# Row sums of the first normalisation, both gelu tiles ahead of the gates, and a series on GpSimd, in an inference step of a hybrid decoder

## Chip, cores and metric

One core of a Trainium2 chip. The metric is the device time of one launch in microseconds (us). Three runs of the kernel before took 2537.53, 2539.8 and 2540.2 us; the median is 2539.8 us.

## The reference

One step of a two-layer decoder trunk for T = 1088 tokens (1024 of a prompt and 8 requests of 8 tokens), D = 1024, everything in float32. Layer 0 is a recurrent block:

```
xn = x * rsqrt(mean(x*x) + eps) * a_norm
gate, xb = split(xn @ w_in)                 # 1024 and 1024 columns
xc = causal depthwise conv of width 4 (xb)
r = sigmoid(xc_block @ gate_r_w[b] + gate_r_b)      # 4 blocks of 256 channels
i = sigmoid(xc_block @ gate_i_w[b] + gate_i_b)
log_a = -8 * r * softplus(-lambda);  a = exp(log_a)
b = sqrt(-expm1(2*log_a)) * (i * xc)
h[t] = a[t] * h[t-1] + b[t]
x = x + (gelu(gate) * h) @ w_out
```

Behind it stand a gated ConvFFN of 3072 channels, a shared K/V projection, a sliding-window attention layer and a second ConvFFN. The change touches the first normalisation and the recurrent block.

## The kernel before

**Layout and products.** x lies transposed in SBUF: 8 tiles of 128 channels by 1088 tokens (`x[:, k, :]`), in three chunks of 384, 384 and 320 tokens. Each float32 product is made of three: weights and data are both split into a rounded part (ScalarE, `Copy` into fp32r, lines 1360, 1365 and 1386) and a remainder (a subtraction on VectorE, lines 1866, 1871 and 1907), and TensorE adds hi x hi, hi x lo and lo x hi (lines 866 to 868). `piece(n, s, c)` is one chunk for 128 output columns, 24 matmuls; `unit(n, s)` is its three chunks. `s` is one of two sides: side 0 has weights `whi[0]`, `wlo[0]` and PSUM banks 0 to 2, side 1 has banks 3 to 5. `n` counts the weights of a side. `prep(n, s)` on ScalarE rounds the weights as soon as the last piece that used the old ones is done; `prep` on VectorE makes the remainder. SP fetches the next raw weights once the remainder is made.

**Queues.** There is no scheduler. Each engine has one hand-written list of instructions with semaphore waits, in which an instruction waits for all ahead of it in its own list. So the place of a `prep` or of a copy in ScalarE's list decides when TensorE gets it.

**Start.** SP loads six tiles of 128 tokens (512 KB each), then 18 small parameter rows, the first two weights (512 KB each), three more token tiles and ten small rows for the FFN. TensorE transposes each token tile in two halves (`set_up`, line 853), ScalarE and VectorE copy the halves alternately into `x` (lines 1354 and 1862). The mean of squares of a chunk is made in parts: ScalarE squares 4 or 6 of its 8 tiles (line 1404), GpSimd adds them (lines 2495 and 2498), VectorE squares and adds the rest (lines 1920 and 1923), and a matmul with a matrix of 1/D adds over the partitions (lines 901 and 903). ScalarE takes the root (line 1379), VectorE the reciprocal (line 1876), both over 128x384. Then for each of the 8 tiles VectorE multiplies x by the gain and the inverse root (line 1899), ScalarE rounds, VectorE subtracts (line 1907), and TensorE's `first_pair` follows tile by tile. The parameter transposes (line 839) and those of the FFN rows (line 845) stand between its pieces.

**A recurrent block c of four** (`lru_block`; blocks 1 and 2 are a loop with the block number in a register). TensorE: the two units of xb (n = 4c, sides 0 and 1), the unit of gate tile 2c (n = 4c+1, side 0), the gates r and i of both halves (four times three pieces of 6 matmuls, 72 together), then the unit of gate tile 2c+1 (n = 4c+3, side 1). ScalarE moves xb into `convin` (line 1444), VectorE makes the convolution (lines 2001 and 2003), ScalarE rounds it and VectorE takes the remainder `xclo` (line 2020), once for each half; both have to be there for the gates. ScalarE then has gelu (line 1462), four sigmoids (line 1482), two tanh (line 1492), two exponentials (line 1498) and two roots (line 1502), VectorE products and the scan (line 2051), and GpSimd the product with gelu (line 2537). Before block 0 VectorE computes softplus of lambda with a series of nine terms on 128x8 (lines 1958 to 1985), and GpSimd writes the history of each convolution into `convin` (line 2506).

**Last block and output projection.** ScalarE takes the last gate tile out of PSUM as it is, and applies gelu later (line 1531). Between the roots it rounds the six finished tiles of z in three chunks (line 1513); VectorE makes the remainders of three tiles of the first two chunks (line 2056), GpSimd the others (line 2526). TensorE runs six of the eight tiles of the output projection for all six banks, then the last two tiles bank by bank (lines 990 to 992). `residual` then adds into x (line 2108), squares, rounds x (line 1556) and only then the next weights.

`first_pair` of the KV and query projections uses a normalisation in which VectorE and GpSimd (line 2470) make the remainders in turn; the change extends this to the first one.

## Time and profile before

| | |
|---|---|
| median of three runs | 2539.8 us |
| the profiled execution | 2541.68 us, span 2539.8 us |
| TensorE matmul | 2477.2 us, 98% of the span, mean granted clock 0.987 |
| VectorE | 1276.9 us, 50% |
| ScalarE | 780.7 us, 31% |
| GpSimd | 250.8 us, 10% |
| DMA | 52 GB/s over the span |

The granted clock is a share of full speed, 2.4 GHz; 0.50 is the lower level, 1.2 GHz. In the profile PE is TensorE's matmul, PEld its weight load, DVE VectorE, ACT ScalarE, POOL GpSimd. A row names line, engine, operation, output <- inputs and shape. In rows by group "x12 | 6.3, 521" is the count, the busy time in us and the mean of one in ns; in rows in order of time the first two numbers are start and busy time in us, and a bracket tells how long the engine had been idle and what released it.

### The profile page before, as it was taken

Reading aid. Unit: us, or ns where it says so; the run is one execution under the profiler, and the core shown is the slowest. Engines: PE = TensorE matmul, PEld = TensorE weight load, DVE = VectorE, ACT = ScalarE, POOL = GpSimd, SP = SyncE. Lnnn points to the kernel's source line nnn. Section 1 sums busy time; section 2 is a strip of 40 time slices with the busy share of each in tenths; the row PEclk is TensorE's granted clock in tenths of the full one; section 3 lists DMA queues with packets and bytes.
Section 4 is the critical chain, followed back from the end, with each engine's and each line's share of the span. In section 5 each row is a group of like instructions: output and inputs, shape, how many; then the busy total and the mean of one; then the engine's idle time right before and its main releaser. Section 6 shows DMA issues by size and latency. Waiting matters only on the chain.

```text
span 2539.8 us, 39942 instructions
## 1 busy us (share of the span) xinstructions
PE 2477.2 (98%) x15280; PEld 2418.2 (95%) x15280; DVE 1276.9 (50%) x2054; ACT 780.7 (31%) x1266; POOL 250.8 (10%) x358
## 2 busy tenths in 40 slices
PE   5899999999999999999999989999999999999999
PEld 4899999999999999999999956999999999999999
DVE  7666645442443444345456667454434524533543
ACT  3554523221221221112334476332112202311221
POOL 2012241000000000000310054310000000000000
PEclk7999989999999999999999999999999999999999
DMA  3111111111111111111164112111111111111113
GB/s 110 38 42 41 50 34 42 50 34 50 50 37 46 50 41 37 54 41 42 50 144 100 49 37 88 42 51 41 37 54 41 36 55 41 41 41 50 46 35 93
DMA packets 227170, 130.89 MB, mean 52 GB/s; under 512 B 24781, under 2 KB 224653, under 8 KB 226860
## 3 DMA queue, kind: packets, MB, share of 16 engines
q1 hardware_dynamic: 224932, 126.47, 17.0%
q10 hardware_dynamic: 2100, 3.37, 1.1%
q8 instruction: 49, 0.80, 0.1%
q14 instruction: 25, 0.20, 0.0%
q0 software_dynamic: 64, 0.05, 0.0%
HBM read 116.76 MB, written 15.01 MB: 52 GB/s over the span
## 4 chain that ended last, share of the span: by engine, by line
PE 93%; DVE 4%; ACT 1%; issue 1%; POOL 0%; DMA 0%; DVEq 0%; ACTq 0%; POOLq 0%
PE ps L866 29%; PE ps L868 29%; PE ps L867 29%; PE ps L1199 1%; PE ps L1251 1%; PE ps L1116 0%; PE ps L901 0%; DVE y L2003 0%; PE ps L1084 0%; PE ps L1109 0%; PE ps L1299 0%; DVE sa L1907 0%; PE ps L1029 0%; PE ps L1301 0%; PE ps L1300 0%
## 5 line engine op out<-in xcount | busy, mean ns | idle before, releaser
L866 PE MATMUL ps<-sa,whi 128*128 128x384 f32 (+1 forms) x1836 | 603.5, 329 | 20.2 <-DVE sa L1907 13.1
L868 PE MATMUL ps<-sa,wlo 128*128 128x384 f32 (+1 forms) x1836 | 601.6, 328 | 0.0
L867 PE MATMUL ps<-sa,whi 128*128 128x384 f32 (+1 forms) x1836 | 601.3, 327 | 0.0
L866 PE MATMUL ps<-sb,whi 128*128 128x384 f32 (+1 forms) x1764 | 582.2, 330 | 0.0
L868 PE MATMUL ps<-sb,wlo 128*128 128x384 f32 (+1 forms) x1764 | 576.5, 327 | 0.0
L867 PE MATMUL ps<-sb,whi 128*128 128x384 f32 (+1 forms) x1764 | 576.1, 327 | 0.0
L1360 ACT ACTIVATE whi<-raw 128x1024 fp32r<-128x1024 f32 (+1 forms) x204 | 201.4, 987 | 836.7 <-PE ps L868 824.2
L866 PEld LDWEIGHTS ps<-sa,whi 128*128 128x128 f32 x1836 | 346.4, 189 | 23.3 <-issue 16.7
L867 PEld LDWEIGHTS ps<-sa,whi 128*128 128x128 f32 x1836 | 346.6, 189 | 0.5 <-issue 0.2
L868 PEld LDWEIGHTS ps<-sa,wlo 128*128 128x128 f32 x1836 | 346.6, 189 | 0.0
L866 PEld LDWEIGHTS ps<-sb,whi 128*128 128x128 f32 x1764 | 332.0, 188 | 2.8 <-issue 1.2
L867 PEld LDWEIGHTS ps<-sb,whi 128*128 128x128 f32 x1764 | 331.9, 188 | 1.4
L868 PEld LDWEIGHTS ps<-sb,wlo 128*128 128x128 f32 x1764 | 331.8, 188 | 0.0
L1866 DVE TENSOR_TENSOR wlo<-raw,whi 128x1024 fp32r<-128x1024 f32 (+1 forms) x204 | 235.0, 1152 | 161.9 <-ACT whi L1360 161.8
L2108 DVE TENSOR_TENSOR x<-ps,x 128x384 f32 (+3 forms) x216 | 115.3, 534 | 382.7 <-PE ps L868 377.5
L866 PE MATMUL ps<-sc,whi 128*128 128x384 f32 (+1 forms) x816 | 266.4, 326 | 2.6 <-DVE sc L1907 2.6
L868 PE MATMUL ps<-sc,wlo 128*128 128x384 f32 (+1 forms) x816 | 265.8, 326 | 0.0
L867 PE MATMUL ps<-sc,whi 128*128 128x384 f32 (+1 forms) x816 | 265.8, 326 | 0.0
L2177 DVE TENSOR_TENSOR convin<-ps,rstd 128x384 f32<-128x384 f32 x144 | 73.3, 510 | 213.6 <-PE ps L868 212.1
L2555 POOL COPY fstash<-convin 128x2 f32 x48 | 8.9, 185 | 1509.6 <-DVE y L2003 1509.6
L866 PEld LDWEIGHTS ps<-sc,whi 128*128 128x128 f32 x816 | 153.3, 188 | 4.5 <-DVE sc L1907 4.3
L867 PEld LDWEIGHTS ps<-sc,whi 128*128 128x128 f32 x816 | 153.2, 188 | 0.1
(338 smaller groups left out, 2596.3 us busy)
## 6 DMA issues: line engine op xcount, KB each, us to landing
raw<-in_f_w_up SPq DMA_DIRECT2D x96, 512.0 KB, 3.8
raw<-in_f_w_down SPq DMA_DIRECT2D x64, 384.0 KB, 3.4
raw<-in_a_w_in SPq DMA_DIRECT2D x16, 512.0 KB, 4.0
x_spill<-x SPq DMA_DIRECT2D x1, 4352.0 KB, 15.4
x<-x_spill SPq DMA_DIRECT2D x8, 544.0 KB, 5.5
xrows<-in_x_prompt SPq DMA_DIRECT2D x8, 512.0 KB, 6.5
raw<-in_a_w_out SPq DMA_DIRECT2D x8, 512.0 KB, 3.7
raw<-in_w_q SPq DMA_DIRECT2D x16, 256.0 KB, 3.6
```

The lines of the kernel that those rows point to most:

```text
L866: pe.matmul(out, whi[s][:, w], mhi[k][:, chunk(c)], start=(k == 0), stop=False)
L867: pe.matmul(out, whi[s][:, w], mlo[k][:, chunk(c)], start=False, stop=False)
L868: last = pe.matmul(out, wlo[s][:, w], mhi[k][:, chunk(c)], start=False, stop=(k == nk - 1))
L1199: last[e] = pe.matmul(out, qz[h0:h0 + HD, 4 * a + j, b * WIN:(b + 1) * WIN], kf[h0:h0 + HD, a, key:key + 256 - k0], start=True, stop=True)
L1251: last = pe.matmul(ps[h0:h0 + HD, 6, :], v, pt_buffer(2 * p + e)[:, h, :], start=(h == 0 or b == 0), stop=(h == 1))
L1360: act.activation(whi[s][:, 0:cols], raw[s][:, 0:cols], ACT.Copy).then_inc(hi_ready[s], 1)
L1866: dve.tensor_tensor(wlo[s][:, 0:cols], raw[s][:, 0:cols], whi[s][:, 0:cols].bitcast(F32), ALU.subtract)\
L2108: ins = dve.tensor_tensor(xt, bank(b, c), xt, ALU.add)
L2177: dve.tensor_tensor(gp[:, FFN_W - 1 + lo:FFN_W - 1 + lo + w], ps[:, c, 0:w], rstd[:, lo:lo + w], ALU.mult)\
L2555: pool.tensor_copy(fstash[:, ds(f, 1), 0:2], gp[:, SEQ:SEQ + 2].rearrange("p (o w) -> p o w", o=1))
```

## The change

*Start.* SP loads token tiles 0 to 2, a_norm as 8 rows of 128 (`anrow`), the first two weights, then token tiles 3 to 8, and the parameter rows behind them. ScalarE squares each token tile where it landed, tokens on partitions, with the sum over its 1024 channels accumulated into one column; a root of three columns and a reciprocal of three columns follow, and TensorE multiplies each column, broadcast to 128, with the identity, which puts the inverse roots of a chunk as a row on all partitions of a PSUM bank. VectorE's multiply reads them there. The remainders of odd tiles go to GpSimd. A first square root on one column loads the table. The transposes of a chunk's tokens stand one chunk ahead of its pieces; those of the FFN rows behind the whole pair.

*Blocks 0 and 3* (`both`). The unit of gate tile 2c+1 moves ahead of the gates (n = 4c+1, side 1). r uses side 0 and i side 1. Each tanh follows its r. Next weights of both sides are prepared in the second half of the gates. In block 3 the roundings of the six finished tiles follow each gelu piece, all 18 remainders are made on GpSimd, and gelu is applied straight from PSUM. The output projection's last two tiles go tile by tile over all banks, and its first residual rounds the next weights ahead of x.

*Series.* VectorE computes only exp(-|lambda|)/(2 + exp(-|lambda|)); GpSimd does the rest in block 0. GpSimd also writes the next block's history ahead of its wait for the second scan.

The diff, cut to its core (`...` marks what is left out):

```diff
+            for tt in range(3):
+                token_rows(tt)
+            eng.dma_start(anrow[:, :], A["a_norm"].rearrange("o (k p) -> (o k) p", p=P)).then_inc(an_in, 16)
+            conv_loads(0)
+            for tt in range(3, 9):
                 token_rows(tt)
             parameter_rows()
...
+            def root_spread(c):
+                pe.wait_ge(in_inv, c + 1)
...
+                for tt in range(3 * c, 3 * c + 3):
+                    w = P if tt < 8 else NS
+                    last = pe.matmul(ps[:, 6 + c % 2, (tt - 3 * c) * P:(tt - 3 * c) * P + w],
+                                     in_sums[0:w, tt:tt + 1].broadcast_to([w, P]), ident[0:w, 0:w], start=True, stop=True)
+                last.then_inc(in_spread, 1)
+            def first_products():
+                set_up(0, SET_END[0])
+                pe.wait_ge(an_in, 16)
+                pe.transpose(ps[:, 7, 0:KD], anrow[:, :], ident[0:KD, 0:KD]).then_inc(an_tr, 1)
+                root_spread(0)
+                set_up(SET_END[0], SET_END[1])
+                for c in range(3):
+                    for s in range(2):
...
+                        def ready(c, k):
+                            if (c, k) == (1, KD - 2):
+                                root_spread(2)
+                            normed(0)(c, k)
+                        piece(0, s, c, KD, split_a, None if s else ready)
+                        if (c, s) == (0, 0):
+                            root_spread(1)
+                            set_up(SET_END[1], SET_END[2] - 2)
...
+                pe.wait_ge(xn_mult, 3 * KD)
+                set_up(SET_END[2] + 2, NSET)
...
                 unit(4 * c + 1, 0, KD, split_a)
+                if both:
+                    unit(4 * c + 1, 1, KD, split_a)
                 pe.wait_ge(xc_lo, 2 * c + 2)
                 for m in range(2):
+                    for s, n in ((0, 4 * c + 2), (1, 4 * c + 2)) if both else ((1, 4 * c + 1), (0, 4 * c + 2)):
...
+            for c in range(3):
+                for s in range(2):
+                    out_part(s, c, range(KD - 2))
+            for k in range(KD - 2, KD):
+                for s in range(2):
+                    for c in range(3):
+                        out_part(s, c, [k])
...
+            def row_squares(tt):
+                w = P if tt < 8 else NS
+                wait(act, sq_done, tt)
+                act.wait_ge(rows_in[tt], 16)
+                act.activation(t1[0:w, 0:D], xrows[0:w, tt, :], ACT.Square, accum_out=in_sums[0:w, tt:tt + 1]).then_inc(sq_done, 1)
...
+            act.activation(spt[:, 0, 0:1], epst[:, 0:1], ACT.Sqrt)
+            row_squares(0)
+            set_up(0, 1)
+            row_squares(1)
+            set_up(2, 3)
+            row_squares(2)
+            row_roots(0)
+            set_up(4, 5)
+            prep(0, 0, KD * P)
             def first_chunk_in(k):
+                if k in (1, 3, 5):
+                    row_squares((k - 1) // 2 + 3)
+                elif k in (2, 4, 6):
+                    set_up(SET_END[0] + k - 2, SET_END[0] + k - 1)
+                if k == 6:
+                    row_roots(1)
+                elif k == 7:
                     prep(0, 1, KD * P)
...
             act.activation(spt[:, 1, :], spt[:, 0, :], ACT.Exp, scale=-1.0).then_inc(sp_exp, 1)
+            set_up(SET_END[2] + 2, NSET)
...
                         if ch == 1:
                             prepare()
+                        if last and s == 1:
+                            highs(ch)
...
                 branch(0, 4 * c + 1, lambda: prep_gates(4 * c + 2, 0))
+                if both:
+                    branch(1, 4 * c + 1, lambda: prep_gates(4 * c + 2, 1))
...
+                if both:
+                    act.wait_ge(sp_done, 2)
...
+                        if both and i == 0:
+                            act.wait_ge(bank_free[s * 3 + 2], n + 1)
+                            tanh(m)
...
-            with act.Fori(0, KD // 2 - 1) as i:
+            residual(N_OUT, 0, 1, C_FN, sb, KD * P, "", weights_first=True)
+            with act.Fori(1, KD // 2 - 1) as i:
...
+                def times(j, out):
+                    return dve.scalar_tensor_tensor(out, x[:, j, chunk(c)], an[:, j:j + 1], bank(6 + c % 2, c),
+                                                    ALU.mult, ALU.mult)
+                norm(0, c, split_a, times, between)
...
+            def softplus():
+                t, t2_, u = spt[:, 0, :], spt[:, 1, :], spt[:, 3, :]
+                pool.wait_ge(sp_ready, 2)
+                seq.mark(pool.tensor_tensor(t2_, t, t, ALU.mult))
+                seq.settle()
...
+                for i in range(terms - 2, -1, -1):
+                    seq.mark(pool.tensor_tensor(u, u, t2_, ALU.mult))
+                    seq.settle()
+                    seq.mark(pool.tensor_scalar(u, u, 1.0 / (2 * i + 1), None, ALU.add))
+                    seq.settle()
```

## Rows read from the trace of the kernel before

**Rows 1.** Waits of TensorE: who for whom; us in total, times, longest

```profile
PE ps L866 <- DVE sa L1907: 13.1, 4, 8.6
...
PE ps L866 <- DVE xclo L2020: 5.0, 1, 5.0
...
PE ps L866 <- DVE wlo L1866: 4.0, 1, 4.0
...
PE ps L866 <- issue: 3.0, 1, 3.0
```

**Rows 2.** Stretches: length; busy us (count) per engine; clock, DMA share, GB/s

```profile
0.00:83.16 83.16, 50.51 (x261) 42.79 (x261) 63.31 (x113) 33.89 (x65) 17.53 (x25) 0.82 0.28 85
83.16:126.50 43.34, 38.35 (x217) 38.09 (x218) 25.84 (x31) 24.99 (x34) 0.54 (x3) 0.92 0.21 56
...
100.22:114.70 14.48, 14.48 (x74) 14.48 (x75) 1.92 (x2) 9.99 (x17) 0.00 (x0) 0.82 0.13 36
281.13:293.00 11.87, 11.87 (x74) 11.87 (x73) 1.92 (x2) 9.08 (x15) 0.00 (x0) 1.00 0.15 44
307.50:341.75 34.25, 25.06 (x132) 23.50 (x130) 25.88 (x23) 15.66 (x26) 22.91 (x19) 0.89 0.05 16
...
341.75:347.60 5.85, 5.85 (x18) 5.85 (x19) 3.03 (x5) 3.37 (x5) 2.82 (x3) 0.50 0.32 90
```

**Rows 3.** TensorE in order of time, 0 to 75 us

```profile
4.57 7.95 PE L853 MATMUL ps<-ident,xrows 128*128 128x128 f32 x48 [4.57 <-DMA xrows<-in_x_prompt]
...
29.84 0.66 PE L866 MATMUL ps<-sa,whi 128*128 128x384 f32 x1 [8.57 <-DVE sa L1907]
```

**Rows 4.** Groups by shape, ScalarE and VectorE, 0 to 170 us (accumulator read: 1500 to 1700)

```profile
L1360 ACT ACTIVATE whi<-raw 128x1024 fp32r<-128x1024 f32 x7 | 7.4, 1058 | 0.6 <-PE ps L868 0.6
L1386 ACT ACTIVATE sa<-y 128x384 fp32r<-128x384 f32 x12 | 6.3, 521 | 12.5 <-DVE y L1899 12.5
...
L1354 ACT ACTIVATE x<-ps 128x512 f32<-128x512 f32 x8 | 4.4, 593 | 3.8 <-PE ps L853 3.8
...
L1815 ACT ACTIVATION_READ_ACCUMULATOR t<-t,stat 128x1 f32 x36 | 6.8, 188 | 0.0
...
L1866 DVE TENSOR_TENSOR wlo<-raw,whi 128x1024 fp32r<-128x1024 f32 x7 | 8.9, 1277 | 12.8 <-ACT whi L1360 12.7
L1862 DVE COPY x<-ps 128x512 f32<-128x512 f32 x8 | 5.2, 678 | 7.0 <-PE ps L853 7.0
...
L1907 DVE TENSOR_TENSOR sc<-y,sc 128x384 fp32r<-128x384 f32 x4 | 2.1, 556 | 6.1 <-ACT sc L1386 6.1
```

**Rows 5.** VectorE and GpSimd in order of time, later normalisation, 1342 to 1347 us

```profile
1342.05 1.61 DVE L1899 SCALAR_TENSOR_TENSOR y<-x,pcol,rstd 128x320 f32<-128x320 f32 x2
...
1345.93 1.12 DVE L2285 SCALAR_TENSOR_TENSOR kf<-kf,qkn,ps 128x384 f32<-128x384 f32 x2
...
1346.26 0.88 POOL L2470 TENSOR_TENSOR sc<-convin,sc 128x320 fp32r<-128x320 f32 x1 [1.00 <-ACT sc L1386]
```

**Rows 6.** ScalarE in order of time, behind the first block's tanh

```profile
118.66 1.28 ACT L1498 ACT_TABLE_LOAD   x1
119.95 1.21 ACT L1498 ACTIVATE t<-t,sp 128x1088 f32<-128x1088 f32 x1
```

**Rows 7.** VectorE in order of time: first convolution, second remainder, second scan of block 0

```profile
82.97 1.03 DVE L2001 TENSOR_SCALAR y<-convin,pcol 128x1024 f32<-128x1024 f32 x2
...
98.87 1.29 DVE L2020 TENSOR_TENSOR xclo<-y,xchi 128x1088 fp32r<-128x1088 f32 x1 [1.18 <-ACT xchi L1455]
...
134.47 2.47 DVE L2051 TENSOR_TENSOR_SCAN z<-z 128x1088 f32<-128x1088 f32 x1
```

**Rows 8.** ScalarE in order of time from 301 us; GpSimd groups by shape, 0 to 350 us

```profile
301.06 2.58 ACT L1513 ACTIVATE sa<-z 128x384 fp32r<-128x384 f32 x6
...
L2526 POOL TENSOR_TENSOR sa<-z,sa 128x384 fp32r<-128x384 f32 x6 | 9.1, 1541 | 37.6 <-ACT sa L1513 37.6
...
L2538 POOL COPY pcol<-z x2 | 2.4, 1194 | 0.0
```

More of the change, by code:

```diff
@@ L234, in build @@
         sp_ready = sem("sp_ready")
+        sp_done = sem("sp_done")
         hist_ready = sem("hist_ready")
@@ L967, in lru_block @@
                             piece(n + m, s, ch, 2, xc_split, k0=2 * m)
[L968 to L971 removed]
+                if not both:
+                    unit(4 * c + 3, 1, KD, split_a)
+            lru_block(0, first=True, both=True)
+            with pe.Fori(1, LRU_BLOCKS - 1) as c:
                 lru_block(c)
[L974 to L994 removed]
@@ new lines, in _, with out_part @@
+            lru_block(LRU_BLOCKS - 1, both=True)
+            def out_part(s, c, ks):
+                if ks[0] == 0:
+                    if c == 0:
+                        pe.wait_ge(hi_ready[s], N_OUT + 1)
+                        pe.wait_ge(lo_ready[s], N_OUT + 1)
+                    pe.wait_ge(bank_free[3 * s + c], N_OUT)
+                for k in ks:
+                    if k < KD - 2:
+                        pe.wait_ge(z_lo_pool, (KD - 2) * c + k + 1)
+                    else:
+                        pe.wait_ge(z_lo, k - (KD - 2) + 1)
+                    w, out = ds(k * P, P), bank(3 * s + c, c)
+                    zhi, zlo = split_a[0][k][:, chunk(c)], split_a[1][k][:, chunk(c)]
+                    pe.matmul(out, whi[s][:, w], zhi, start=(k == 0), stop=False)
+                    pe.matmul(out, whi[s][:, w], zlo, start=False, stop=False)
+                    last = pe.matmul(out, wlo[s][:, w], zhi, start=False, stop=(k == KD - 1))
+                if ks[-1] == KD - 1:
+                    last.then_inc(bank_ready[3 * s + c], 1)
@@ L1388, in norm_hi @@
                             between(k)
[L1389 to L1392 removed]
+                if chunks[-1] == 2:
                     act.wait_ge(xn_lo, lo_base(u + 1))
[L1395 to L1405 removed]
@@ L1444, in evac_conv, with lru_block @@
                     act.activation(gp[:, hist + lo:hist + lo + w], ps[:, b, 0:w], ACT.Copy).then_inc(bank_free[b], 1)
-            def lru_block(c, last):
+            def lru_block(c, first=False, last=False):
+                both = first or last
                 for s in range(2):
@@ L1455, in lru_block, with highs @@
                     act.activation(xchi[:, s, :], y[:, :], ACT.Copy).then_inc(xc_hi, 1)
+                def highs(ch):
+                    for k in range(KD - 2):
+                        act.wait_ge(z_ready, k + 1)
+                        act.activation(split_a[0][k][:, chunk(ch)], z[:, k, chunk(ch)], ACT.Copy).then_inc(z_hi, 1)
                 def branch(s, n, prepare):
@@ L2009, in conv, with lru_block @@
                         seq.settle()
-            def lru_block(c, last, start):
+            def lru_block(c, start, first=False, last=False):
+                both = first or last
                 seq.at = start
@@ L2530, in lru_block @@
                     h = gate_tiles(c, m)[1]
+                    if m == 1 and not last:
+                        conv_history(kt + 1)
                     pool.wait_ge(scan_done, kt + 1)
```

542 lines of the change are left out of this document (231 added, 311 removed).

## The prediction

> **What bounds the kernel now.** I began with the share of busy time (given above): TensorE at 98%, so what can be won is only its idle time, about 62 us, and its time at half clock. TensorE's waits say where the idle time lies [rows 1]: the longest are all in the first 102 us, plus two around the output projection of the recurrent block. The stretches show the clock [rows 2]: 0.82 on average up to 83.16 us, 0.82 again in the gates of the first block, 0.50 for 5.85 us behind the gap that ends at 341.75 us, and 1.00 where nothing waits. Of 72 small-operand matmuls, a unit or a block's gates, one takes 11.87 us at full clock (74 records there), so 0.165 us each; at half clock 0.325 us (18 in 5.85). Three stalls matter. (a) From 12.5 to 29.84 us TensorE has almost no work: the transposes of rows 0 to 5 end at 12.5 us and the first product starts at 29.84 us [rows 3]; between them lie squares, adds, a ones-matmul, root and reciprocal. Up to 80 us it goes on in pieces (13.1 us of waits for split tiles). (b) It waits 3.0 us at 79.9 us (the weight split stands on VectorE behind the softplus series) and 5.0 us at 95.2 us for the second half of the convolved input, then runs at half clock. (c) From 307.5 to 341.75 us TensorE is busy for 25.06 of 34.25 us at 0.89: 9.2 us idle, 3.8 us of clock, and 2.9 us of clock behind it, some 16 us.
>
> **Part 1, first normalisation.** It removes the squares by tile, their adds, the ones-matmuls and the wide reciprocals, and puts in nine row squares with accumulation, small roots and reciprocals, and nine 128-column matmuls that spread the inverses. No row shows a 128x1024 square with accumulation. Lower bound: the 128x1024 copy, 1.06 us; upper: that plus twice the accumulator read of 0.19 us [rows 4]. I take 1.25 us. No row has the multiply with the inverse in PSUM. Next to it: a DVE operation of this kind with a PSUM operand took 0.56 us beside a running GpSimd subtraction, while with both operands in SBUF it took 0.80 us in the same surroundings (two in 1.61 us, and of 320 columns only) [rows 5]. I take 0.56 and keep 0.8 for the range.
> The chain, from the durations of [rows 4]: row 0 lands at 4.5 us as now; three squares (3.75) and two copies (1.2) on ScalarE, roots, reciprocals and spread (0.9): the inverses are there at 10.3 us. Weights are queued ahead of rows 3 to 8; at one 512 KB tile in 1.33 us, which is what 48 transposes in 7.95 us imply, row 5 lands near 14 us, which hides. VectorE's chunk 0 is 8 multiplies, 4 subtractions, 2 weight splits of 1.23 us and 3 copies of 0.68 us: 11.2 us. ScalarE has 8x0.52 + 3x1.25 + 3x0.59 + 2x1.06 = 11.8 us. They alternate, so about 13.6 us: chunk 0 is done at 24 us. TensorE has to do all transposes of rows 3 to 5 before its first piece, and two of these hang on copies that stand at tiles 2 and 3 of the chunk: first product at 17.5 us, 12 us sooner than now. I let it run at half clock for 5 us, like behind other gaps. Piece to 24.5, spread and four transpose jobs (3.2), second piece 4.0: 31.5 us. Chunk 1 starts at 25 us and is bound by ScalarE (9.7 us and its waits): 36 us. TensorE: 37, then 41.3 us; the third chunk is done by 43-45 us, and two pieces of 320 columns with the parameter transposes end at 49.6, the f transposes at 51.3 us. Then a tail that the change itself makes: ScalarE copies those transposes only then (0.6 us), moves the convolution's input out of PSUM (four copies, 0.4 us each), and rounds the next weights (1.06); VectorE splits them (1.2); with 0.1 us for each hand-over 4 us behind 51.3. Second unit at 55.3 us; now it starts at 83.16 us. For subtractions that still collide with GpSimd I add 1 us: 56.3. **Term A: -26.9 us.** The moved DMAs cost nothing here: the parameter rows are wanted at 41 us, and the queue would have issued them by 14 us.
>
> **Part 2, series on GpSimd and both gelu tiles ahead.** The second unit is followed by the other gelu unit, so 23.7 us of matmuls cover both convolutions, which took from 82.97 to 100.16 us [rows 7]. Their 5.0 us wait and the half clock behind it go. From the second unit to the end of gates and both gelu units it is 43.3 us now (83.16 to 126.5), then 3 x 11.87 = 35.6. **Term B: -7.7 us.** The series on GpSimd: 23 dependent small operations from about 64 us. Below: 0.19 us plus a hand-over of 0.1, 7 us; above: 1.19 us each, as a one-column copy takes beside a busy VectorE [rows 8], 27 us. The first sigmoid wants it at 81 us. VectorE is idle in parts of that stretch, so I take 12 us: hidden, 5 us to spare. At the upper bound it would cost 10 us.
> **What is late next.** The gelu unit that stood behind the gates covered the scans. Now the next block's units follow at once. Its gates start 35.6 us after these gates end. VectorE's chain: second scan ends at 136.9 us, 22.2 us behind the gates' end at 114.7 [rows 7]; the tanh tiles now lie between the sigmoids, so the exponential starts 2.9 instead of 5.25 us behind [rows 6]: 19.8. Weight split 1.2, then two convolutions as at 82.97 to 100.16, 17.2 us: 38.2 us, and 0.6 for register-addressed operations. **Term C: +3.2 us** of wait; the bounds are 0 (the whole chain 3 us shorter) and 8 (another 2 us, and half clock behind it). I add 1 us for the clock.
>
> **Part 3, last block.** ScalarE now has the roundings of six tiles behind each gelu piece: 2.58 us for six [rows 8]. The rounding of the gate weights stands ahead of the second group and waits for the unit's end, 11.9 us, so the groups end at 17.8 us from the unit's start, the sigmoid table and first sigmoid at 19.7; the third set of gates waits 2.0 us for its bank. Behind the gates 1.4 us for the first weights and 0.7 for the second. GpSimd has all 18 subtractions, at 1.54 us beside VectorE [rows 8] 28 us, wanted piece by piece up to 39.6 us: hidden. The scan chain gives the seventh tile at 49.1 us, when six tiles' products (17.8 us) have ended at 45.6: 3.5 us idle and 2.3 us of half clock. The eighth tile is ready when wanted. With rounding of the weights first, the next unit starts about 1 us behind. Sum: 47.4 us of matmuls and 12.7 us of loss, 60.1 us. Now: 60.6 us (281.13 to 341.75) and 2.9 us of half clock behind it, 63.5. **Term D: -3.4 us.**
> On this chain lie table loads. The row shows 1.28 us, and the exponential begins 0.01 us behind it [rows 6]. The Trainium skill (ScalarE: Activation LUTs, What ACT_TABLE_LOAD costs) counts a drain of 1.38 us on top of each load, 2.66 us in all. By that rule the sigmoid and exponential loads of this chain would add 2.8 us and the sum would end at 2508.8 us; the trace does not agree, so I don't take it.
>
> **Sum.** -26.9 - 7.7 + 3.2 + 1 - 3.4 = -33.8 us. The profiled execution took 2541.7 us, which gives 2507.9; that execution lies 1.9 us above the median of the runs, 2539.8, and set against the median the change gives 2506.0 us, which I forecast. A measurement of this kernel tells 0.2%, 5 us, from no change.
>
> **Rivals.**
> *The start is less loose than drawn* (0.20). Multiplies are stretched to 0.8 us, squares take 1.44 us, and the pieces of the first chunk wait more: 24 x 0.24 + 9 x 0.19 = 7.5 us, and the second unit's clock falls back once more, 3 us; with term C at its upper bound 4 more. -19 us: 2521. For it: beside GpSimd the multiplies of the later normalisation are stretched [rows 5]. Against: their second operand will be in PSUM, and ScalarE, not VectorE, sets the second chunk.
> *Handover and last block go smoothly* (0.17). No wait at the second block's gates and no half clock in the last block: 4.2 + 2.3 us, and the first allowance of 1 us: -41 to -46, 2498 to 2494.
> *Slower: the clock never comes back while the start is in pieces* (0.04). Place: TensorE from 17.5 us to the gates of the first block. At 0.325 instead of 0.165 us a matmul the first pair ends 25 us later and the two units take 23.7 us more: -33.8 + 48.7 = +15 us, 2555. It decides once about 34 us' worth of full-clock work is done at half clock. Against it: behind 341.75 us half clock ended after 5.85 us, and the first block's gates got 0.82 in the mean [rows 2].
> *It doesn't do what it says* (0.05): the transposes ahead of the first piece, or the series, hold the first sigmoid as long as the old chain did, 10 us for the series and 15 for the transposes: -9 us, 2531.
> The forecast's own case has 0.54 (2500 to 2512). The range 2493 to 2521 leaves out the slow case, the one in which it does not do what it says, and the ends of the others. Faster by over 0.2%: 0.94; within: 0.02; slower: 0.04.
>
> **What would show it.** In the changed profile: first product near 17.5 us and second unit near 56 us (A); no wait for the convolved input in the first block (B); a new wait of 2 to 5 us of TensorE for it near 127 us, at the second block's gates (C); near 296 us two waits under 4 us at the last tiles of the output projection, and the next weights' wait down from 4.0 to about 1 us (D). Wrong if the first piece starts past 22 us, if the sigmoid waits for the series, or if half clock fills the first 50 us.

## The result and the profile after

The changed kernel took 2509.9 us in the median of 4 runs (2507.7 to 2510.4) where the kernel before took 2539.7 us in the same comparison: a ratio of 0.9885, 95% interval 0.9872 to 0.9897. The profiled execution took 2509.8 us with a span of 2507.9 us, 31.9 us less than the span before. The forecast was 2506.0 us, with 2493 to 2521 as its range. The sum is close; the terms in it are not all right.

TensorE's waits of the changed kernel, the answer to [rows 1] (us in total, times, longest):

```profile
PE ps L873 <- DVE xclo L2031: 6.2, 1, 6.2
PE ps L1281 <- DVE pt L2392: 5.8, 11, 1.6
PE ps L860 <- DMA xrows<-in_x_prompt: 5.6, 2, 4.6
PE ps L873 <- DVE wlo L1903: 4.5, 2, 3.3
PE ps L1012 <- DVE sc L2102: 2.7, 1, 2.7
PE ps L873 <- ACT t L1544: 1.8, 1, 1.8
```

The 13.1 us for split tiles are gone, and so is the 5.0 us wait for the convolved input in block 0. A larger one of the same kind, 6.2 us, has come at block 1's gates. The 4.0 us for weights at the end of the recurrent part have become 1.2, but the same line now also has 3.3 us in front of the second unit.

The stretches of the changed kernel, to set against [rows 2]. The cuts are the second unit's start, block 1's start, the new wait, what follows it, and the last block from its second unit to the handover:

```profile
0.00:54.38 54.38, 43.03 (x267) 39.34 (x268) 31.05 (x68) 33.24 (x68) 14.05 (x22) 0.96 0.43 134
54.38:91.42 37.04, 37.04 (x217) 37.04 (x217) 19.62 (x24) 18.37 (x30) 10.71 (x26) 0.96 0.16 44
91.42:127.16 35.74, 35.74 (x218) 35.48 (x216) 30.76 (x31) 15.67 (x22) 11.01 (x12) 1.00 0.12 35
127.16:133.35 6.19, 0.00 (x1) 0.03 (x1) 4.49 (x7) 2.64 (x3) 0.00 (x0) 0.92 0.19 56
133.35:139.20 5.85, 5.85 (x19) 5.85 (x20) 0.69 (x1) 3.88 (x7) 0.00 (x0) 0.50 0.32 92
139.20:255.40 116.20, 116.20 (x703) 115.74 (x703) 78.07 (x81) 61.00 (x85) 23.05 (x24) 1.00 0.14 41
255.40:312.24 56.84, 51.13 (x288) 50.14 (x288) 29.98 (x29) 33.14 (x54) 25.89 (x26) 0.94 0.14 38
```

Read down the clock column: 0.96 in the start where it was 0.82, full between the losses, 0.50 for 5.85 us behind the new wait. Over the whole span the mean granted clock is 0.993 where it was 0.987. Every wait below has such a tail behind it or is spared one, and that decides what the edits are worth to within 2 to 4 us.

**The start** goes as drawn. TensorE in order of time, the answer to [rows 3]:

```profile
18.06 0.42 PE L873 MATMUL ps<-sa,whi 128*128 128x384 f32 x1
...
54.38 0.66 PE L873 MATMUL ps<-sa,whi 128*128 128x384 f32 x1 [3.31 <-DVE wlo L1903]
```

and the groups by shape up to 54 us, the answer to [rows 4, 5]: the row squares took 1.05 us and an accumulator read of 0.19, and the multiplies with their inverse in PSUM 0.60 us, also beside GpSimd's subtractions:

```profile
L1426 ACT ACTIVATE t<-xrows 128x1024 f32<-128x1024 f32 x8 | 8.4, 1048 | 2.2 <-DMA xrows<-in_x_prompt 2.2
...
L1939 DVE SCALAR_TENSOR_TENSOR convin<-x,an,ps 128x384 f32<-128x384 f32 x8 | 4.7, 603 | 0.0
```

**The new wait** is read on VectorE and GpSimd. VectorE in order of time from the second scan of block 0 to the second remainder of block 1, to set against [rows 7]:

```profile
103.27 0.17 DVE L2063 TENSOR_TENSOR t<-t,h0a 128x8 f32<-128x8 f32 x1
...
107.12 2.40 DVE L2063 TENSOR_TENSOR z<-z,h0a 128x8 f32<-128x8 f32 x1
109.55 2.47 DVE L2065 TENSOR_TENSOR_SCAN z<-z 128x1088 f32<-128x1088 f32 x1
111.95 1.19 DVE L1903 TENSOR_TENSOR wlo<-raw,whi 128x1024 fp32r<-128x1024 f32 x1
113.06 3.26 DVE L2011 TENSOR_SCALAR y<-convin,pcol 128x1024 f32<-128x1024 f32 x2
...
124.74 1.03 DVE L2011 TENSOR_SCALAR y<-convin,pcol 128x1024 f32<-128x1024 f32 x2
...
131.82 1.29 DVE L2031 TENSOR_TENSOR xclo<-y,xchi 128x1088 fp32r<-128x1088 f32 x1 [1.18 <-ACT xchi L1496]
```

GpSimd in the same stretch:

```profile
105.98 3.50 POOL L2581 TENSOR_TENSOR z<-z,t 128x1088 f32<-128x1088 f32 x1 [31.41 <-DVE t L2065]
...
109.69 2.34 POOL L2519 COPY convin<-pcol 128x24 f32<-128x24 f32 x1
112.10 3.44 POOL L2581 TENSOR_TENSOR z<-z 128x1088 f32<-128x1088 f32 x1
```

An operation on 8 columns takes 0.17 us at 103.27 and 2.40 us at 107.12, and ends at 109.52, when GpSimd's product of the first z tile and its scan (from 105.98, 3.50 us) has just ended at 109.48. Two operations of the first convolution take 3.26 us at 113.06, beside the second product, and 1.03 us at 124.74, when GpSimd is idle. The first of these collisions was there before the change (2.39 us at 132.05 us). The second is new: VectorE used to have nothing but a weight split there (1.63 us beside the product, at 139.92 us), and now has the next convolution. Not only VectorE waits: GpSimd's 24-column copy at 109.69 takes 2.34 us and ends with VectorE's scan. The Trainium skill (SBUF — State Buffer, Who interferes with whom) says that VectorE and GpSimd share one port pair under an exclusive lock: a VectorE operation with two SBUF inputs contends for it with a GpSimd operation that reads SBUF, as one in a two-port mode does, and whichever comes later waits for the other to end. The trace agrees to 0.04 us at 109.5.

**The last block** has the forecast waits: 1.8 us for the gates' bank, 2.7 us for the seventh tile, 1.2 us for the next weights. ScalarE's table load is as in [rows 6]:

```profile
93.73 1.28 ACT L1562 ACT_TABLE_LOAD   x1
95.03 1.21 ACT L1562 ACTIVATE t<-t,sp 128x1088 f32<-128x1088 f32 x1
```

It is again 1.28 us, and the exponential again begins 0.02 us behind its end. The drain of 1.38 us that the prediction weighed, from the Trainium skill (ScalarE: Activation LUTs, What ACT_TABLE_LOAD costs), is not seen here either.

### The profile page after: what moved, and what is told of

Same layout as the page of the kernel before. It is cut to its first block, busy times and chain, and to the rows that moved or that the text cites. A ratio compares the mean times of both kernels' runs of the same rounds, so it can differ in the third digit from the quotient of the medians.

```text
span 2507.9 us, 39872 instructions
## 1 busy us (share of the span) xinstructions
PE 2468.2 (98%) x15287; PEld 2414.3 (96%) x15287; DVE 1238.4 (49%) x2003; ACT 780.2 (31%) x1269; POOL 268.4 (11%) x384
## 4 chain that ended last, share of the span: by engine, by line
PE 93%; DVE 3%; ACT 2%; issue 1%; POOL 0%; DMA 0%; DVEq 0%; ACTq 0%; POOLq 0%
PE ps L873 29%; PE ps L875 29%; PE ps L874 29%; PE ps L1229 1%; PE ps L1281 1%; PE ps L1146 0%; PE ps L1329 0%; PE ps L1139 0%; PE ps L1331 0%; PE ps L1330 0%; PE ps L1059 0%; PE ps L1114 0%; PE ps L860 0%; DVE pt L2392 0%; DVE y L2374 0%
```

## Experiments

All runs start from the changed kernel. The kernel before, timed beside each group of them, took 2537.4, 2540.3 and 2537.5 us in the median, so ratios and spans are what to compare. "Second unit" is where TensorE starts it, "wait" the longest between it and the last block, "restart" the end of the gates' wait in the last block, "handover" the first product behind the recurrent output projection; all in us of the profiled executions. In seven of the rows (changed, changed again, block 0 old, both tiles ahead everywhere, no second z product, residual in old order, last tiles bank by bank) the code up to the second unit is the same, and it starts between 53.58 and 54.85 us: a difference of about 1 us there says nothing. No run puts the old sums of squares back. The largest term of the gain, the start, is therefore read from the two traces and not shown by undoing it.

| kernel | second unit | wait | restart | handover | span | ratio to before, 95% interval |
|---|---|---|---|---|---|---|
| changed | 54.38 | 6.2 | 275.01 | 312.24 | 2507.9 | 0.9885 (0.9872 to 0.9897) |
| changed, again | 54.53 | 6.2 | 275.54 | 312.85 | 2508.3 | 0.9890 (0.9875 to 0.9905) |
| block 0 old | 54.85 | 3.5 | 271.74 | 309.11 | 2504.9 | 0.9870 (0.9854 to 0.9887) |
| both tiles ahead everywhere | 53.58 | none | 267.81 | 305.30 | 2502.5 | 0.9862 (0.9846 to 0.9879) |
| FFN copies later | 51.29 | 6.2 | 270.57 | 307.72 | 2503.4 | 0.9863 (0.9845 to 0.9880) |
| no second z product | 54.51 | 4.0 | 271.80 | 308.95 | 2504.6 | 0.9864 (0.9847 to 0.9880) |
| both tiles everywhere, FFN copies later | 51.37 | none | 263.22 | 300.69 | 2494.5 | 0.9836 (0.9823 to 0.9850) |
| series on VectorE | 57.34 | 6.4 | 278.65 | 316.05 | 2509.0 | 0.9893 (0.9878 to 0.9908) |
| residual in old order | 54.10 | 6.2 | 274.75 | 314.27 | 2514.2 | 0.9892 (0.9877 to 0.9907) |
| last tiles bank by bank | 53.67 | 6.2 | 274.74 | 316.26 | 2510.9 | 0.9896 (0.9881 to 0.9912) |
| block 0 old, FFN copies later | 51.84 | 5.0 | 269.94 | 305.84 | 2501.4 | 0.9863 (0.9848 to 0.9878) |
| rows ahead of weights | 59.92 | 6.2 | 280.73 | 318.18 | 2513.8 | 0.9911 (0.9898 to 0.9925) |
| all remainders on VectorE | 55.39 | 6.4 | 275.48 | 311.38 | 2504.3 | 0.9882 (0.9867 to 0.9897) |

**Block 0 in its old order.** The theory was that the 6.2 us wait is the price of moving block 0's second tile, the rival that the convolution is late for itself.

```diff
-            lru_block(0, first=True, both=True)
+            lru_block(0, first=True)
...
-                both = first or last
+                both, tiles = last, False
```

> Block 0 keeps the order of the kernel before (one gelu tile ahead of its gates, the other behind), while the start with sums per token from the rows, the series on GpSimd and the last block stay as in the changed kernel. Theory (the 6.2 us wait for the conv remainder at block 1's gates, with its clock, is the price of moving block 0's second tile ahead): that wait is gone, TensorE waits before block 0's gates again, some 5 us with 3 us of clock behind it, and the time is that of the changed kernel within 3 us (2507 to 2513). Rival (the wait at block 1's gates has another cause, the late start of the second convolution on VectorE beside GpSimd): it stays at 3 us or more, and the time is 2516 or more.

The wait at block 1's gates is gone; in its place TensorE waits 3.5 us before block 0's gates, with half clock for some 3 us behind it. TensorE's waits between 50 and 255 us in this kernel:

```profile
PE ps L873 <- DVE xclo L2034: 3.5, 1, 3.5
PE ps L873 <- DVE wlo L1906: 3.3, 1, 3.3
```

The theory holds: moving block 0's second tile ahead of the gates took away a wait of 3.5 us and made one of 6.2. The wait is smaller than the 5 us expected, and the time of 2505.4 us lies 1.6 us under the expected range. The ratios, 0.9870 and 0.9885, have intervals that overlap, but the stretches tell the two kernels apart: from the second unit to the restart it takes 216.9 us and not 220.6. With the other parts of the change in place, this part is a loss of some 3 us.

**Both tiles ahead in all four blocks.** If only the cover in block 1 is short, a fourth unit in front of its gates should end the wait.

```diff
             with pe.Fori(1, LRU_BLOCKS - 1) as c:
-                lru_block(c)
+                lru_block(c, both=True)
```

(the same for the loads, and ScalarE's and VectorE's preparations one unit earlier)

> The changed kernel with both gelu tiles ahead of the gates in all four recurrent blocks. Theory (the VectorE chain of two scans and two convolutions, some 42 us behind block 0's gates, is only covered by the 35.6 us that three units of block 1 take; with a fourth unit the cover is 47.4 us): no wait over 1 us at block 1's gates, no half clock at 127 to 140 us, and 2499 to 2502 us. Rival (the waits are carried to the next block, where the gated product now comes later): the wait at block 1 goes but waits of 2 us or more stand in blocks 1 to 3, and the time is 2506 or more.

TensorE's waits between 50 and 255 us:

```profile
PE ps L873 <- DVE wlo L1903: 3.3, 1, 3.3
PE ps L873 <- issue: 0.7, 2, 0.5
```

No wait for the convolved input is left in any block, and from the second unit to the restart it takes 214.2 us where the changed kernel takes 220.6. The time of 2504.1 us is 2 us above what was expected. Two things took back some of it: the clock stayed low longer behind the unchanged 3.3 us wait at 53.6 us (2.6 us lost in place of 1.4), and from the restart to the end it takes 1.8 us more, with a wait of 1.0 us in front of the output projection that the changed kernel doesn't have.

**FFN copies later.** The copies of the transposed FFN rows are moved behind the rounding of the second unit's weights, on both engines (ScalarE shown).

```diff
-            set_up(SET_END[2] + 2, NSET)
...
                     else:
                         prep_gates(n + 1, 1)
+                    if first and s == 0:
+                        set_up(SET_END[2] + 2, NSET)
```

> The changed kernel with the copies of the transposed FFN rows on ScalarE and VectorE moved behind the rounding of the second unit's weights. Theory (the 3.3 us that TensorE waits for the second unit's weight remainder at 54.4 us are these two copies ahead of the eviction and the rounding): that wait is 1.5 us or less, the second unit starts at 52 to 53 us in place of 54.4, and with the later waits standing relative to block 0's gates all of it is kept: 2506.5 to 2508.5 us. Rival (VectorE has something else in front of the remainder, the last product of the start): the wait stays at 3 us and the time at 2509 to 2511.

The second unit starts at 51.29 us, 0.7 us behind the last transposes, and no half clock follows. That is 3.1 us sooner, more than expected, since the eviction of the first unit no longer waits for the FFN transposes either (it begins at 47.74 and not at 50.83 us). The wait alone accounts for 2.6 us of it, 0.7 in place of 3.3. At the restart it is 4.4 us ahead, 1.3 us of it for the clock that doesn't fall. The 6.2 us wait stays as it is: it stands relative to block 0's gates, so the gain passes through it. The median of 2502.9 us lies 3.6 us under the expected range; the four runs are scattered from 2500.6 to 2508.2 us.

**No second z product.** GpSimd multiplies only 1 of 1088 columns of block 0's second z tile by its scan; the rest of that product is left out.

```diff
-                        pool.tensor_tensor(zt, zt, h, ALU.mult).then_inc(z_ready, 1)
+                        n_col = 1 if first and m == 1 else T
+                        pool.tensor_tensor(zt[:, 0:n_col], zt[:, 0:n_col], h[:, 0:n_col], ALU.mult).then_inc(z_ready, 1)
```

> The changed kernel in which GpSimd multiplies only 1 of 1088 columns of block 0's second z tile by its scan (the rest of that product is left out, so the output differs). Theory (the second z product runs beside block 1's first convolution on VectorE and stretches one of its operations from 1.0 to 3.3 us): the operation is back at 1.0 to 1.3 us, the wait for the conv remainder falls from 6.2 to 3.5 to 4.5 us, and the time by 2 to 3 us to 2507 to 2508. Rival (the convolution is late for its history copy or its inputs and not for GpSimd): the wait stays within 0.5 us of 6.2, the time at 2509 to 2511.

VectorE in order of time in this kernel:

```profile
109.67 2.48 DVE L2065 TENSOR_TENSOR_SCAN z<-z 128x1088 f32<-128x1088 f32 x1
112.07 1.19 DVE L1903 TENSOR_TENSOR wlo<-raw,whi 128x1024 fp32r<-128x1024 f32 x1
113.18 1.03 DVE L2011 TENSOR_SCALAR y<-convin,pcol 128x1024 f32<-128x1024 f32 x2
```

The same two operations take 1.03 in place of 3.26 us, and the wait is 4.0 in place of 6.2 us: 2.2 us in both places. The other 4.0 us are the chain without any new collision against its cover. The rival would have left the wait alone. The time of 2503.6 us lies 3.4 us under the expected range: the edit spares 2.2 us of waiting and 1.2 us of half clock behind it (1.7 in place of 2.9).

**Both edits together.** This is the version that the first four runs point to.

> The changed kernel with both gelu tiles ahead of the gates in all four blocks and the copies of the transposed FFN rows behind the second unit's weights. Theory (the two losses are separate): the second unit starts at 51 to 52 us at full clock, block 1's gates don't wait, and the span is 2507.9 less 3.1 (start), 1.7 (clock behind the start), 9.6 (wait and clock at block 1) plus 2.8 us (small waits at blocks 2 and 3 and in the last block, as the kernel with both tiles ahead everywhere showed): 2496.3, a time of 2496 to 2499 us. Rival (VectorE's chain now binds in blocks 2 and 3 instead): waits of 2 us or more there, and 2501 us or more.

The mean granted clock and the waits between 50 and 255 us:

```profile
core 0: 2494.5 us, clock 0.996
```

```profile
PE ps L873 <- issue: 1.5, 3, 0.7
```

The two losses are separate. The median of 2498.3 us is as expected. The ratio of 0.9836 (0.9823 to 0.9850) lies below the whole interval of the changed kernel, and the span is 13.4 us shorter; of these, 11.8 us are there at the restart. Against the kernels with one of the two edits the intervals just touch, but the restart comes 4.6 and 7.4 us sooner.

**Series on VectorE.** The softplus series is put back where it was.

```diff
-                if first:
-                    softplus()
```

(GpSimd; VectorE gets the series, in 22 operations, ahead of the second unit's weight split)

> The changed kernel with the softplus series back on VectorE, right behind its argument and ahead of the copy of the FFN rows. Theory (GpSimd took it off the path of the second unit's weights): 23 operations of 0.17 to 0.20 us with hand-overs, 5 us from 49.0 us, so VectorE splits the weights at 55 instead of 53.05 us and the second unit starts at 56.2 to 56.8 instead of 54.4 us: 2 to 4 us more in all, 2511 to 2514. Rival (VectorE had those 5 us idle anyway, since the FFN rows' copy only starts at 51.1 us): under 0.5 us later, and the time within 1.5 us of the changed kernel.

The remainder of the weights is split at 56.02 us, and the second unit starts at 57.34 us, 3.0 us later, behind a wait of 6.2 us in place of 3.3. VectorE's operations took 0.17 us each and 4.2 us in all; on GpSimd they took 12.1 us (62.48 to 74.57), with nobody waiting, as the first sigmoid began at 82.13 us. The span is only 1.1 us longer, since it takes 2.7 us less from the handover to the end, where one stretch of half clock is missing that the changed kernel has at 1542 us. By the second unit and the handover, which are 3.0 and 3.8 us later, the part is worth some 3 us.

**The residual in its old order.** The next weights are rounded behind the first sums again.

```diff
-            residual(N_OUT, 0, 1, C_FN, sb, KD * P, "", weights_first=True)
-            with act.Fori(1, KD // 2 - 1) as i:
+            with act.Fori(0, KD // 2 - 1) as i:
```

> The changed kernel with the first residual of the recurrent block's output projection in the old order (the next weights rounded behind the first sums and not ahead). Theory: TensorE waits 3.5 to 4.0 us instead of 1.2 us for the next weights' remainder near 312 us, with up to 2 us of half clock behind it: 2.5 to 5 us more, 2511 to 2515. Rival (the sums take the weights' place on the path, since the residual has to be done for the next normalisation): the wait grows, but a wait further on shrinks by as much, and the time is within 1.5 us of the changed kernel.

The wait is 3.4 us and not 1.2, and from restart to handover it takes 39.5 us and not 37.2. Behind the longer wait the clock fell, which it hadn't done behind 1.2 us. The span is 6.3 us longer: 2.0 us are there at the handover, and 4.3 come behind it, 2.8 of these for the clock right behind the wait. The time of 2513.9 us is within the expected, but this was the slowest of four executions (2510.8 to 2516.1), and the ratios differ by only 0.0007. From restart to handover the order is worth 2.3 us.

**The last two z tiles bank by bank.**

```diff
-            for k in range(KD - 2, KD):
-                for s in range(2):
-                    for c in range(3):
-                        out_part(s, c, [k])
+            for c in range(3):
+                for s in range(2):
+                    out_part(s, c, range(KD - 2, KD))
```

> The changed kernel with the products of the last two z tiles taken bank by bank, both tiles of a bank together, as before, and not tile by tile over all six banks. Theory (in the new order the 18 products of the seventh tile cover the wait for the eighth): behind the 2.7 us wait for the seventh tile TensorE waits a second time, 2.5 to 3.2 us, near 304 us, and the time is 2 to 5 us longer, 2511 to 2515. Rival (half clock behind the first wait hides it): the second wait is under 1 us and the time within 1.5 us.

TensorE behind the first six tiles:

```profile
302.57 0.44 PE L1012 MATMUL ps<-sc,whi 128*128 128x384 f32 x1 [2.81 <-DVE sc L2101]
306.24 0.69 PE L1012 MATMUL ps<-sc,whi 128*128 128x384 f32 x1 [2.88 <-DVE sc L2101]
```

The second wait is there with 2.88 us, and from restart to handover it takes 4.3 us more. The time of 2512.6 us is within the expected. The 18 products of the seventh tile do hide the eighth.

**Block 0 old and FFN copies later.** Do the two gains add up?

> The changed kernel with block 0 in its old order (one gelu tile ahead of the gates) and the copies of the transposed FFN rows behind the second unit's weights. Theory (the two edits are independent): the span of the kernel with block 0 in its old order, 2504.9, less 3.1 to 3.5 us for the earlier second unit and 0 to 2 us of clock behind it, plus 0.6 us for the copies that now stand in VectorE's way to the convolved input: 2499 to 2502 us, and a wait of 3.5 to 4.5 us at block 0's gates. Rival (the gain at the start is lost in the wait at block 0's gates, since VectorE's convolutions don't move): that wait is 6 us or more and the span 2504 or more.

The span of 2501.4 is within the expected, but the wait before block 0's gates grew from 3.5 to 5.0 us, more than forecast: TensorE comes to it 4.5 us earlier (3.0 from the start, the rest from a clock that doesn't fall), the convolved remainder only 3.0 us. With both tiles ahead that chain is covered, and the version above is 6.9 us shorter.

This run also explains why the wait was 3.5 us with block 0 in its old order and 5.0 us in the kernel before. From the second unit's start to the end of that chain it takes 17.0 us in all three. What differs is the time of the 72 matmuls in front of the gates; before, block 0 old, and this kernel:

```profile
83.16:95.23 12.07, 12.07 (x72) 11.80 (x72) 10.24 (x15) 2.78 (x6) 0.54 (x3) 1.00 0.21 58
54.85:68.42 13.57, 13.57 (x72) 13.31 (x72) 11.70 (x17) 2.78 (x6) 5.26 (x12) 0.88 0.23 60
51.84:63.94 12.10, 12.09 (x72) 11.83 (x72) 10.85 (x16) 2.77 (x6) 3.99 (x10) 1.00 0.21 61
```

At full clock TensorE comes to the gates 12.1 us behind the start of the unit and waits 5.0 us; at half clock behind the 3.3 us wait it comes there 1.5 us later and waits 3.5. The half clock behind one wait was taken off the next.

**Rows ahead of weights.** The moved loads had been costed at nothing. Here rows 3 to 8 are queued ahead of the first two weight tiles.

```diff
-            conv_loads(0)
             for tt in range(3, 9):
                 token_rows(tt)
+            conv_loads(0)
             parameter_rows()
```

> The changed kernel with the loads of token rows 3 to 8 queued ahead of the first two weight tiles. Theory (the order of the queue decides the start): the first weights land some 6 us later, ScalarE, which rounds them at 9.8 us, stands in front of its first tiles until 13 to 14 us, and the first product starts at 19.5 to 21.5 us in place of 18.1; the second unit starts 1 to 3 us later. Rival (the transposes of rows 3 to 5 set the first product, and they come sooner): it starts at 17.5 us or before and the second unit at 54 us or before.

ScalarE in order of time:

```profile
9.30 0.58 ACT L1384 ACTIVATE x<-ps 128x512 f32<-128x512 f32 x1
16.98 1.06 ACT L1390 ACTIVATE whi<-raw 128x1024 fp32r<-128x1024 f32 x1 [7.11 <-DMA raw<-in_a_w_in]
```

ScalarE stands 7.1 us in front of the weights, twice what was expected. The first product starts at 23.94 us, past the 19.5 to 21.5 us of the theory, and the second unit 5.5 us later where 1 to 3 had been expected. In the change the weights stay ahead of these rows, so nothing was lost there. The order is worth 5.5 us all the same.

**All remainders on VectorE.**

```diff
-            for c in range(3):
-                norm_lo(0, c, split_a)
```

(GpSimd; VectorE takes the odd tiles' remainders too)

> The changed kernel with all 24 remainders of the first normalisation on VectorE and none on GpSimd. Theory (ScalarE with its roundings, squares and copies sets the chunks, as forecast): 12 more subtractions at 0.56 us, 2.2 us in each chunk, are hidden for the larger part, the second unit starts within 1.5 us of 54.4 us and the time is within 2 us of the changed kernel. Rival (VectorE, 8.3 us busy in each 10 us between 10 and 30 us, sets the chunks): the second unit starts 2 to 6 us later, at 56.5 to 60.5 us, and the time is 2512 to 2516 us.

The second unit starts 1.0 us later than in the changed kernel and 0.9 us later than in its control. That is within the theory, and so small that kernels with the same start differ by as much (53.58 to 54.85 us): whether GpSimd's twelve subtractions save anything in the start is not shown. The rival is out. The time came out 2.8 us *shorter* than the control's, outside what either theory gave, and the clock has a part in it. From 270 to 282 us and from 300 to 312 us in this kernel:

```profile
270.00:282.00 12.00, 9.86 (x59) 9.36 (x58) 4.14 (x3) 11.90 (x23) 12.00 (x12) 1.00 0.17 44
300.00:312.00 12.00, 7.60 (x43) 6.83 (x42) 8.50 (x8) 4.30 (x6) 5.00 (x7) 1.00 0.00 1
```

The same stretches of the changed kernel run again beside it:

```profile
270.00:282.00 12.00, 10.21 (x53) 9.97 (x52) 3.43 (x3) 11.33 (x23) 12.00 (x12) 0.86 0.15 44
300.00:312.00 12.00, 8.95 (x45) 8.42 (x43) 8.48 (x10) 2.89 (x5) 3.70 (x7) 0.86 0.01 1
```

TensorE waited 1.8 and 2.8 us in the one and 1.8 and 2.7 us in the other, at the same places. In the control the clock fell behind both waits, in this kernel behind neither: 0.14 of 24 us, 3.4 us in all. Only part of it is saved, since TensorE then stands idle for 4.0 and not 2.7 us in the output projection: from restart to handover it takes 35.9 in place of 37.3 us. Another 2.5 us of the 4.0 by which the spans differ lie behind the handover, where the control has a stretch of half clock at 1542 us that this kernel lacks (3.4 us). The code there is the same.

**The changed kernel again,** as a control.

> The changed kernel itself, beside the others of this call: 2508 to 2511 us, the waits of 3.3 us at 54 us and of 6.2 us at 133 us again.

All its waits are the same to 0.1 us, the second unit starts within 0.2 us, the spans differ by 0.4 us, and the median of 2510.0 us is within the expected.

## Why the prediction was right, and where it was not

Against the spans the terms read as follows. "Measured" is the difference between the stretches of the two kernels.

| term | forecast | measured |
|---|---|---|
| A, start of the second unit | -26.9 | 54.38 - 83.16 = -28.8 |
| B, to the start of block 1 | -7.7 | 37.04 - 43.34 = -6.3 |
| C, to the second unit of the last block | +4.2 | 163.98 - 154.63 = +9.4 |
| D, last block and the clock behind it | -3.4 | 56.84 - 60.62 - 2.9 = -6.7 |
| the rest | 0 | +0.5 |
| sum | -33.8 | -31.9 |

**A held nearly step by step.** Forecast and seen: first product 17.5 and 18.06 us, first chunk with its two weight splits done 24 and 23.8, second 36 and 34.7, third 43 to 45 and 44.6, end of the FFN transposes 51.3 and 51.1, a tail of 4 and 3.3 us. The durations taken between far bounds were right, too: 1.25 us for a row square with its read (1.24), 0.56 us for the multiply with PSUM (0.60). The allowance of 1 us for collisions was hardly used. From 24.1 to 51.1 us TensorE stood idle for only 0.3 us, so its own work set the end of the start, and the early second chunk changed nothing. Two steps were not as drawn. The half clock of 5 us at the first product didn't come: TensorE is at full clock from 18.06 us, and the fall lies ahead of it (0.54 from 12.7 to 16.0 us). The terms of the tail add up to 4.5 us and some hand-overs, and not to 4; it took 3.3 because ScalarE began its copy 0.7 us before the last transposes ended, and moved the convolution's input in 1.3 and not 1.6 us. The 1.9 us by which A was too cautious are the allowance (1.0), the tail (0.7) and 0.2 us at the end of the transposes; the same start scatters by about 1 us in other executions, so the agreement is no closer than that. The queue was right, for the reason that the run with the rows first shows: the weights stay in front. What the prediction called a tail "that the change itself makes" was right as a mechanism, but it was taken as a fixed cost. The run with the later copies shows that 2.6 us of it were a matter of order, and the clock behind it too.

**B failed on one step:** that the stretch runs at full clock. Its row has 0.96 over 37.04 us, 1.5 us, since the clock fell behind the 3.3 us tail of A. The 5.0 us wait and its half clock are gone as forecast. The series took 12.1 us on GpSimd where 12 was taken, hidden; the 12 had been picked between the bounds of 7 and 27 us and not worked out, so that it fits is luck. Putting the series back on VectorE costs 3 us at the second unit.

**C is the term that was mis-sized.** The cover of 35.6 us was right (35.74). The failing step is "VectorE's chain: ... 38.2 us, and 0.6 for register-addressed operations". It ended 41.7 us behind the gates: the second scan at 20.6 and not 19.8, since the exponential began 3.6 and not 2.9 us behind the gates, and the first convolution 2.2 us longer than in the rows of before. So the wait was 6.2 and not 3.2 us. The prediction took the convolution's duration from [rows 7], where GpSimd was idle, and moved it into a stretch where GpSimd multiplies. The run without the second z product shows those 2.2 us. On the clock 1 us had been allowed and 2.9 us came (5.85 us at 0.50). The whole, 9.4 us by the stretches, lies above the stated upper bound of 8. That the cover is what is short is shown by the run with both tiles ahead everywhere, in which the wait is gone.

This has a consequence that the prediction did not see, because it costed the parts only against the kernel before. For block 0 the move of the second tile was counted as B's gain (5.0 us of wait and the clock behind it) less C (4.2). Beside the kernel with that part undone, the move loses 3.0 us of span, and 3.7 us between the second unit and the restart. With the rest of the change in place, the wait to be won was 3.5 us and not 5.0, because the start's new tail had put half clock in front of it: without that tail, in the run with block 0 old and the FFN copies later, it is 5.0 us again. With the FFN copies later the move still loses 2.4 us from the second unit to the handover, though the two ratios are then the same (0.9863).

**D was too cautious by 3.3 us.** The three named waits were forecast at 2.0, 3.5 and 1 us and measured at 1.8, 2.7 and 1.2. Two steps failed. One is "Behind the gates 1.4 us for the first weights and 0.7 for the second": TensorE goes from the gates into the output projection with no such wait in the changed kernel. The other is the sum itself: the losses that the prediction names (2.0, 1.4, 0.7, 3.5, 2.3 and 1) make 10.9 us, and it adds 12.7 to the 47.4 us of matmuls, so that 1.8 us have no term behind them. The seventh tile came at 48.1 us of the stretch and not 49.1. Half clock was forecast at 2.3 and cost 3.4 us (0.94 of 56.84), half of it right behind the first wait, where none had been drawn. The two edits that were forecast to matter do: the order over six banks is worth 4.3 us, rounding the weights first 2.3 us, and 2.8 us of clock behind it in the profiled execution.

The errors of C (+5.2) and of A and D (-5.2) cancel, so the sum's 1.9 us come from B and the rest. The forecast time is 3.9 us off the median, since the profiled execution of before lay 1.9 us above the median of its runs and that of after at the median of its own. That the sum is so close is therefore in part luck. None of the rivals came true as a whole. One price named in "The start is less loose than drawn" was paid in full all the same, "term C at its upper bound", while the start that this rival doubted came sooner than forecast. The fast rival's end of -46 us has no terms behind it; those that it names give -41.3.

What stays open: why the same wait is followed by half clock in one kernel and not in the next. No run here controls it.

## What to carry to other kernels

A duration is a property of an operation and of what GpSimd does beside it: when a step moves, look up what the other engine will be doing at its new place, and take its duration from a row with that neighbour. When work is moved in front of a wait, ask whom it used to cover; here a tile taken from behind block 0's gates shortened the cover of the next block's chain, and moving the tile in all blocks took the wait away. Cost each part of a change against the kernel with all its other parts, because what one part can win depends on what the others leave: half clock behind one wait shortened the next by 1.5 us.

## What the runs showed that was not expected

- An operation on 8 columns of 128 partitions on VectorE took 2.40 us in place of 0.17 us, for it ended 0.04 us behind a GpSimd product that had started 1.1 us earlier. GpSimd's 24-column copy took 2.34 us in place of 0.21 in the same way, behind a VectorE scan. The 128x384 multiply with one operand in PSUM was not stretched beside GpSimd's subtractions (0.60 us).
- Of GpSimd's 23 dependent 8-column operations 16 took 0.19 to 0.24 us, the others 0.56 to 1.14 us beside VectorE's splits, remainder and convolution: 12.1 us in all, with hand-overs. VectorE did the series, in 22, in 4.2 us.
- Half clock is less regular than the wait ahead of it. Behind the same 3.3 us wait in front of the second unit it cost 1.4 to 1.7 us in six executions, 2.1 us with all remainders on VectorE, 2.6 us with both tiles ahead everywhere and 2.8 us with the last tiles bank by bank. Behind the waits of 1.8 and 2.7 us in the last block it cost 1.7 us each or nothing. Behind the 1.2 us at the handover it never fell, though in the start it did behind a wait of 1.05 us that followed other idle time (12.70 us). What it costs is not always added to the time: between restart and handover, 3.4 us of it made 1.4 us. Kernels that differ by less than about 4 us of 2500 are therefore told apart by their stretches, not by their spans.
